# A two-layer encoder on one core: input products of two scan steps issued as one group in three rotating PSUM banks, scan outputs gathered in one bank that is copied out first

## What is computed

```
for i in range(2):
    h = rmsnorm(x, g_mix[i]); z = h @ w_in[i]
    u, q, k, v = split(z)
    y_ssm = ssm_mixer(u, ...)        # 32 channel groups, one 64-dim complex state each
    y_att = diff_attention(q, k, v, ...)   # 4 heads, two softmax maps each
    x = x + concat([y_ssm, y_att]) @ w_out[i]
    h = rmsnorm(x, g_ffn[i])
    x = x + (swiglu(h) if i == 0 else moe_swiglu(h))     # top 2 of 8 experts
return rmsnorm(x, g_final)

def ssm_mixer(u, ...):
    y = u * d_skip
    for direction, reverse in ((0, False), (1, True)):
        bu = einsum('blgh,gph->blgp', u, b_bar)           # input products
        states = associative_scan(a*, bu, reverse)        # complex, diagonal
        y = y + real(einsum('blgp,ghp->blgh', states, c)) # outputs
    y = gelu(y)
    y = y * sigmoid(y @ w_glu + b_glu)
    return rmsnorm(y, g_out)
```

## Time and profile before

| | us |
|---|---|
| Median of 3 runs | 1440.24 (1438.28 to 1445.99) |
| Span of the profiled execution | 1437.0 |
| PE busy | 1348.0 (94%) |
| DVE busy | 875.8 (61%) |
| ACT busy | 694.7 (48%) |
| POOL busy | 135.4 (9%) |
| DMA, mean over the span | 303 GB/s |

### The profile page before, as it was taken

How to read it: one execution, slowest core, us unless ns; L and a number is a source line. 1 busy time by engine, 2 the same in 40 slices (tenths; PEclk the granted TensorE clock), 3 DMA queues, 4 the chain that set the end, 5 groups by cost and what they waited for, 6 DMA issues and landing times.

```text
span 1437.0 us, 19125 instructions
## 1 busy us (share of the span) xinstructions
PE 1348.0 (94%) x7246; PEld 980.9 (68%) x7246; DVE 875.8 (61%) x1138; ACT 694.7 (48%) x1023; POOL 135.4 (9%) x111
## 2 busy tenths in 40 slices
PE   6996889999899779899999999999999999999996
PEld 6865558888787555776766667676766666666663
DVE  6888754454398875666565665555665555665552
ACT  4568443434246863445454544454444444444442
POOL 0455200000006640000000000000000000000000
PEclk9997999999899889899999999999999999999999
DMA  8541325443643126699999999999999999999993
GB/s 347 173 171 34 126 106 215 177 175 124 265 125 117 63 66 236 258 411 390 410 421 421 421 421 419 410 421 422 420 422 421 408 420 421 421 421 420 421 421 164
DMA packets 66329, 435.58 MB, mean 303 GB/s; under 512 B 8192, under 2 KB 14720, under 8 KB 16576
## 3 DMA queue, kind: packets, MB, share of 16 engines
q1 hardware_dynamic: 64848, 429.60, 74.4%
q0 software_dynamic: 1392, 4.78, 1.0%
HBM read 429.11 MB, written 2.10 MB: 300 GB/s over the span
## 4 chain that ended last, share of the span: by engine, by line
PE 73%; DMA 9%; DVE 9%; ACT 5%; SPq 2%; issue 2%; ACTq 0%; DVEq 0%
PE ps L2208 19%; PE ps L2243 11%; PE ps L2194 9%; PE ps L2096 7%; PE ps L1863 6%; PE ps L2225 6%; PE ps L2075 4%; DMA raw<-wmoe 4%; DMA first_ring<-wmoe 4%; PE ps L2001 2%; PE ps L1978 2%; SPq L548 2%; DVE raw L1321 1%; PE ps L1901 1%; PE ps L1989 1%
## 5 line engine op out<-in xcount | busy, mean ns | idle before, releaser
L2096 PE MATMUL ps<-wsplit,xh 128*128 128x512 f32 (+1 forms) x352 | 111.4, 388 | 5.0 <-DVE hv L1388 3.4
L1398 DVE TENSOR_TENSOR low_raw<-raw,last_uppers 128x2048 fp32r<-128x2048 f32 x39 | 89.2, 2289 | 38.5 <-ACT last_uppers L839 38.5
L1398 DVE TENSOR_TENSOR low_first<-first_ring,first_uppers 128x2048 fp32r<-128x2048 f32 x31 | 70.8, 2291 | 37.8 <-ACT first_uppers L839 37.8
L2243 PE MATMUL ps<-raw,hn 128*64 128x256 f32 x784 | 92.4, 382 | 0.0
L1863 PE MATMUL ps<-hT,mixw 128*128 128x256 f32 x384 | 89.4, 394 | 3.1 <-DMA mixw<-wmix 2.2
L1398 DVE TENSOR_TENSOR low_raw<-raw,first_uppers 128x2048 fp32r<-128x2048 f32 x31 | 70.8, 2289 | 32.6 <-ACT first_uppers L839 32.6
L1668 DVE TENSOR_TENSOR hv<-hv,ps 128x256 f32<-128x256 f32 x56 | 23.6, 421 | 105.3 <-ACT hv L989 105.3
L1362 DVE TENSOR_TENSOR wsplit<-raw,wsplit 128x2048 fp32r<-128x2048 f32 x33 | 74.5, 2289 | 20.1 <-ACT wsplit L798 20.1
L1863 PEld LDWEIGHTS ps<-hT,mixw 128*128 128x128 f32 x384 | 75.0, 198 | 15.2 <-issue 2.5
L2243 PE MATMUL ps<-last_ring,hn 128*64 128x256 f32 x704 | 83.2, 382 | 0.0
L989 ACT ACTIVATE hv<-ps 128x256 f32<-128x256 f32 x56 | 21.5, 384 | 127.5 <-PE ps L2208 127.5
(11 more groups left out here) (352 smaller groups left out, 3013.0 us busy)
## 6 DMA issues: line engine op xcount, KB each, us to landing
raw<-wmoe SPq DMA_DIRECT2D x148, 1024.0 KB, 22.4
first_ring<-wmoe SPq DMA_DIRECT2D x95, 1024.0 KB, 23.4
last_ring<-wmoe SPq DMA_DIRECT2D x91, 1024.0 KB, 23.2
raw<-wdense SPq DMA_DIRECT2D x33, 1024.0 KB, 5.0
mixw<-wmix SPq DMA_DIRECT2D x12, 2048.0 KB, 8.3
cyt<-bmat SPq DMA_DIRECT2D x2, 2048.0 KB, 12.1
cw<-cmat SPq DMA_DIRECT2D x2, 2048.0 KB, 18.4
qk<-wglu SPq DMA_DIRECT2D x2, 1024.0 KB, 5.0
```

Source lines behind the costliest of these rows:

```text
L1398: tt(lows[at], ring[at], uppers[k % UPPERS].bitcast(F32), ALU.subtract).then_inc(s["lo_done"], 1)
L2096: ins = mm(to, x2[:, fx, t * P:(t + 1) * P], of, start=(fx == 0 and i == 0), stop=(fx == KT - 1 and i == 2))
L2243: ins = mm(to, xlight[:, m % 2, fx], of[:, :, q * P:(q + 1) * P], start=(fx == 0), stop=(fx == KT - 1), tile_position=(0, LCAP * q))
```

## The change

The input products of steps i + 1 and i + 2 are issued as one group in the odd loop steps, and within it the matmuls alternate between the row halves. The scan's products rotate over banks 0, 1 and 2 by the step counted over both layers. All outputs gather in bank 3 (`y_sum`). `gelu_in` raises a new semaphore `y_taken` with the copy, PE waits for it before the next block, and the other operations of `gelu_in` and `gelu_out` read the copy `yt`.

```
--- before.py
+++ after.py
@@ -366,7 +366,7 @@
 
         names = """in_x0 in_x1 in_cst in_par in_b in_c in_glu in_wr out_done unit_done emptied_act emptied_dve act_chain
             dve_chain sumsq rstd hn_ready small_act small_dve cw_ready phase_ready frac_ready trig_ready bu_ready
-            bu_read bu_turned ri_ready scanned summed c_done gin gtanh g_ready gss_done gss_root qs_ready
+            bu_read bu_turned ri_ready scanned summed c_done y_taken gin gtanh g_ready gss_done gss_root qs_ready
             score_ready sums_ready diag_ready normed cat_ready hi_done lo_done piece_done silu_done
             hv_ready turned hid_hi hid_lo dense_added lg_done routed_exp ex_done gain_in sel_ready pos_done
             tagged rows_tagged tables_ready order_ready final_ready products in_d u_zero in_ush in_usw lamb_ready in_yq in_yq_last in_id
@@ -440,6 +440,12 @@
                     step(j, turns - 1, *order[j])
                 for j in range(2 + 6 * turns, 3 * self.n):
                     step(j, 0, *order[j])
+
+        def scan_bank(n):
+
+            return n % 3
+
+        y_sum = ps[:, 3, 0:SEQ]
 
         def gate_bank(c):
             return 1 if c == 1 else 0
@@ -1277,26 +1283,25 @@
             def gelu_in(l, ft):
 
                 dve.wait_ge(s["c_done"], GP * l + 4 * (ft + 1))
-                y = ps[:, 2 + ft % 2, 0:SEQ]
-                link(nc.vector.tensor_copy(yt[:, ft], y))
-                link(tt(th[:, ft], yt[:, ft], y, ALU.mult))
+                nc.vector.tensor_copy(yt[:, ft], y_sum).then_inc(s["y_taken"], 1)
+                dve.wait_ge(s["y_taken"], FT * l + ft + 1)
+                link(tt(th[:, ft], yt[:, ft], yt[:, ft], ALU.mult))
                 link(ts(th[:, ft], th[:, ft], 0.044715, 1.0, ALU.mult, ALU.add))
-                tt(th[:, ft], th[:, ft], y, ALU.mult).then_inc(s["gin"], 1)
+                tt(th[:, ft], th[:, ft], yt[:, ft], ALU.mult).then_inc(s["gin"], 1)
 
             def gelu_out(l, ft):
 
                 dve.wait_ge(s["gtanh"], FT * l + ft + 1)
-                stt(th[:, ft], th[:, ft], 1.0, ps[:, 2 + ft % 2, 0:SEQ], ALU.add, ALU.mult).then_inc(s["g_ready"], 1)
+                stt(th[:, ft], th[:, ft], 1.0, yt[:, ft], ALU.add, ALU.mult).then_inc(s["g_ready"], 1)
 
             def rotate_in(l, i):
 
                 n = GP * l + i
-                b = i % 2
                 dve.wait_ge(s["trig_ready"], n + 1)
                 dve.wait_ge(s["bu_ready"], n + 1)
                 if n:
                     dve.wait_ge(s["ri_ready"], n)
-                bu = ps[:, b].rearrange("p (r t) -> p r t", r=2)
+                bu = ps[:, scan_bank(n)].rearrange("p (r t) -> p r t", r=2)
                 tt(ri2[:], bu[:, ::-1, :], trig[:, n % 3, 1:3, :], ALU.mult).then_inc(s["bu_read"], 1)
                 dve.wait_ge(s["bu_read"], n + 1)
                 tt(bu, bu, trig[:, n % 3, 0:1, :].to_broadcast([P, 2, SEQ]), ALU.mult).then_inc(s["bu_turned"], 1)
@@ -1305,7 +1310,7 @@
 
                 n = GP * l + i
                 dve.wait_ge(s["bu_turned"], n + 1)
-                bu = ps[:, i % 2].rearrange("p (r t) -> p r t", r=2)
+                bu = ps[:, scan_bank(n)].rearrange("p (r t) -> p r t", r=2)
                 tt(bu, bu, ri2[:], ALU.add).then_inc(s["ri_ready"], 1)
 
             def scan(l, i):
@@ -1319,7 +1324,7 @@
                     for r in range(2):
                         c = r * SEQ + d * NCH
                         ins = nc.vector.tensor_tensor_scan(st[:, n % 3, r, d * NCH:(d + 1) * NCH], decay,
-                                                           ps[:, i % 2, c:c + NCH], 0.0, ALU.mult, ALU.add)
+                                                           ps[:, scan_bank(n), c:c + NCH], 0.0, ALU.mult, ALU.add)
                 ins.then_inc(s["scanned"], 1)
 
             def score(l, h, m):
@@ -1877,19 +1882,22 @@
                             ins = nc.tensor.transpose(ps[:, bank(u), at:at + P], bt[:, k, r, d], ident)
                     ins.then_inc(s["unit_done"], 1)
 
-            def bu(l, i):
+            def bu_pair(l, i):
 
                 n = GP * l + i
-                if n >= 2:
+                if n:
                     pe.wait_ge(s["scanned"], n - 1)
-                k, q = i // 2, 64 * (i % 2)
+                k = i // 2
                 for d in range(2):
-                    u = ush[q:q + 64, k, NCH:0:-1] if d else ush[q:q + 64, k, 0:NCH]
                     for r in range(2):
                         c = r * SEQ + d * NCH
-                        ins = mm(ps[:, i % 2, c:c + NCH], bw[q:q + 64, k, r, d, :], u, start=True, stop=True,
-                                 tile_position=(q, 0))
-                ins.then_inc(s["bu_ready"], 1)
+                        for b in range(2):
+                            q = 64 * b
+                            u = ush[q:q + 64, k, NCH:0:-1] if d else ush[q:q + 64, k, 0:NCH]
+                            ins = mm(ps[:, scan_bank(n + b), c:c + NCH], bw[q:q + 64, k, r, d, :], u, start=True, stop=True,
+                                     tile_position=(q, 0))
+                            if d == 1 and r == 1:
+                                ins.then_inc(s["bu_ready"], 1)
 
             def local(l, d):
 
@@ -1907,9 +1915,9 @@
                 n = GP * l + i
                 k = i // 2
                 ft, c = k // 2, k % 2 * NCH
-                if i % 4 == 0 and FT * l + ft >= 2:
-                    pe.wait_ge(s["g_ready"], FT * l + ft - 1)
-                mm(ps[:, 2 + ft % 2, c:c + NCH], loc[:, k, :], usw[:, k, :], start=True, stop=False)
+                if i % 4 == 0 and FT * l + ft:
+                    pe.wait_ge(s["y_taken"], FT * l + ft)
+                mm(y_sum[:, c:c + NCH], loc[:, k, :], usw[:, k, :], start=True, stop=False)
                 pe.wait_ge(s["summed"], n + 2)
                 for d in range(2):
                     for r in range(2):
@@ -1918,7 +1926,7 @@
                             a = ro[:, b, 0, r, d * NCH:(d + 1) * NCH]
                             if d:
                                 a = a[:, ::-1]
-                            ins = mm(ps[q:q + 64, 2 + ft % 2, c:c + NCH], cw[:, r, 2 * (i + b) + d, :], a, start=False,
+                            ins = mm(y_sum[q:q + 64, c:c + NCH], cw[:, r, 2 * (i + b) + d, :], a, start=False,
                                      stop=(d == 1 and r == 1), tile_position=(0, q))
                             if d == 1 and r == 1:
                                 ins.then_inc(s["c_done"], 1)
@@ -2110,16 +2118,15 @@
                     project(l, unit(l, "zu", k), chunk(l, 0), k)
                 turn_b(l)
                 for i in range(STEPS):
-                    if 0 < i < GP - 1:
-                        bu(l, i + 1)
+                    if i % 2 and i < GP - 1:
+                        bu_pair(l, i + 1)
                     for stage, _ in beside(i):
                         if stage[:4] == "zqkv":
                             zqkv(l, int(stage[4:]))
                             if stage == "zqkv0":
                                 empty_wait(unit(l, "bt", PAIRS - 1))
                                 pe.wait_ge(s["in_ush"], 128 * (l + 1))
-                                bu(l, 0)
-                                bu(l, 1)
+                                bu_pair(l, 0)
                         elif stage[:3] == "loc":
                             pe.wait_ge(s["cw_ready"], l + 1)
                             local(l, int(stage[3:]))
```

19 lines of the change are left out of this document (9 added, 10 removed).

## The result

| us | before | after |
|---|---|---|
| Median (lowest to highest) | 1439.26 (1437.15 to 1445.99), 4 runs | 1456.84 (1453.27 to 1461.05), 4 runs |
| The profiled execution | 1437.0 span | 1452.0 span (1453.95 in all) |

The ratio is **1.0116, 95% interval 1.0083 to 1.0149**: slower, and outside the predicted range. The forecast was 1442.9 us.

The account below looks back on a forecast made before the run. PE was taken to bound the scan's first stretch, DVE alternating with ACT the second. Layer 0 at +1.1 us and layer 1 at +1.6 gave +2.7: span 1439.7 us, median 1442.9, range 1434 to 1450.

Parts of the forecast that it names:

- Pairs in turn: Scan's input products: alternating row halves, 1.05 us a pair; first block complete 2.4 us earlier in layer 0, 1.9 in layer 1.
- a microsecond of PE is worth a microsecond in the first stretch: Layer 0's scan, 42 to 80 us: the chain of waits runs only through PE, so PE time counts fully.
- One output bank: Scan outputs: PE's wait for the previous block's copy costs nothing, since the copy comes first by 3 us.
- SBUF inputs, first block: First block's gelu_in on DVE: operations with two SBUF inputs wait for POOL's, 4.55 us instead of 1.94, +2.6 us.
- Second and third block: gelu_in beside POOL: second block meets only the end of POOL's last operation, +0.2 us; third block +1.0 after DVE idle.
- I let a shift at its end go through one for one: End of the scan, both layers: work behind it starts when it ends, so a shift there counts fully.
- nothing in the second: Layer 0's scan, 80 to 151 us: DVE and ACT alternate in the chain, so PE time counts for nothing.
- All meetings are full: Rival: DVE's chain meets POOL's three operations fully, 8.2 us a layer, +12.1 in all, 1452.3 us; chance 0.20.
- The locks cost nothing: Rival: DVE gets through between POOL's operations, only PE's gain counts, -4.3 us, 1435.9 us; chance 0.18.
- the halves do not overlap: Rival: input-product pairs stay at 1.68 us, gain 1.0 in each layer, sum +5.0, 1445.2 us; chance 0.10.

Follow-up runs that it names:

- the first experiment: The changed kernel with square and last product of gelu_in reading the PSUM output bank again, PE waiting for gelu_in's end; 1440.86 us, ratio 1.0013.
- the filled kernel: The changed kernel with five useless matmuls in PE's waits, three before the first head output, two before the first output projection, each layer; 1452.17 us, ratio 1.0058.

## Why the prediction was wrong, step by step

- **Pairs in turn: right.** 16 records in 1.16 us, taken as 1.05 between bounds of 1.02 and 1.68. The first copy came 2.3 us earlier in layer 0 (predicted 2.4), with the 0.40 us wait for scan 2 that was expected. In layer 1 it was 2.6 without the clock (predicted 1.9): the scans were not waited for, since PE was late by then. But the faster first pair let PE reach the local weights before DVE had folded them (0.67 us idle in layer 1, none before), which the prediction did not look at. That "a microsecond of PE is worth a microsecond in the first stretch" did not hold for that pair.
- **One output bank: right.** PE waited nowhere for `y_taken`.
- **SBUF inputs, first block: right.** The chain took 4.37 us, predicted 4.55: +2.4 where I had +2.6. In the phase operation 0.3 came back as expected (0.69 us instead of 0.95), and `gelu_out` met nothing. The Trainium skill (SBUF — State Buffer, "Who interferes with whom") states that a DVE instruction with two SBUF inputs contends with a GpSimd instruction that reads SBUF. The trace agrees: with two SBUF inputs the square took 1.16 us, with one of them in PSUM 0.42.
- **Second and third block: mis-sized.** Second +0.6 (predicted +0.2): it met POOL's last operation, as forecast, but all of it. Third +2.4 before idle time is taken off (predicted +1.5): POOL's step came to start together with the copy, at 136.60 against 136.59. The three blocks together cost 5.4 us, and the stages still grew by only 3.2 and 3.0 us against the 3.5 forecast. Some of the rest is DVE's idle time (0.31 and 0.22 us, as forecast), and some is meetings that fell away: in layer 0 the phase operation at 132.82 us took 1.57 us before and 0.67 after, and the head norm's product 1.00 and 0.69. That the sum came out near is partly luck.
- **"I let a shift at its end go through one for one", and PE's time worth "nothing in the second": this failed.** Without the clock the sum would have been +1.7 us (-4.9 + 6.2 + 0.4), against +2.7 predicted. The clock added 13.3. A stage that grew by 3.2 us did not cost just that: PE's wait at the head norm grew from 1.42 to 3.09 us in layer 0 and from 1.54 to 3.17 in layer 1, and the groups behind it ran partly at half clock, 6.8 us in all. In layer 1 a wait of 0.67 us before the local weights went with another 6.5. And a delay of 4.7 us ahead of layer 1 is not just 4.7: with no lock it cost 13.9. (At 7.1 and 10.1 us the one for one does hold in the kernel before.) The trace of before had the warning: a granted clock of 0.88 in the second stretch of the earlier trace rows, to which I gave no price, and 16.19 us for the first 64 projections of layer 1, where later ones took 7.17 us for 32. What sets the clock at one place and not at another with the same wait stays open.
- **Rivals.** "All meetings are full" gave 1452.3 us and lies nearest to the 1456.84 measured, but that is luck. Its meetings were to cost 8.2 us a layer and cost about 3; the rest was clock. "The locks cost nothing" fell with the first experiment, "the halves do not overlap" with the 1.16 us.

## What to carry to other kernels

Before a DVE operand moves from PSUM to SBUF, look at whether POOL runs beside it: each operation of a chain then waits out one of POOL's (here 0.42 us became 1.2 to 1.4). And price a change of DVE's pace by what PE does behind its waits for DVE, not by the shift alone: where the profile shows the same matmuls at two paces, such as 64 projections in 16.19 us and 32 in 7.17, the clock is in play, and a range must have room for both at every such group. A part of a change that was right in itself (here 4.9 us of PE time) is then not seen in the median.

## What was not expected of the hardware

- A delay of 2.4 us ahead of layer 1 cost 11.3 us, one of 7.1 us only 7.4.
- A group that had been partly at half clock before (16.19 us) could run at full clock (14.05), and the kernel got slower by it: the next groups waited longer for DVE and then took 12.7 to 13.8 us instead of 7.36.
- Three filling matmuls of 2.74 us in a wait of about 3 us gave 1.7 us back at the first head output; with two more in front of the output projection, that one took 1.7 us less as well.
- In the Trainium skill (TensorE: Matmul & The Clock Gate, "HAM oscillation — how this bites in real kernels") waits between groups of matmuls are what brings the clock down again and again (there, waits for DMA). The table above agrees for both places, with one exception; the output projection (2.03 us) and the dense part of layer 0 (3.39 us) had the same wait end both ways.
- What stays open is what makes the same wait end now at full and now at half clock: 2.03 us before the output projection, 3.39 us in the dense part, or 1.1 us before the local weights of layer 0 (1.10 with the inputs in PSUM, 1.11 in the filled kernel). No run here separates it.
